# First loads of a hybrid decoder step: sample and shift rows requested by ScalarE, first weights behind the prompt rows, eight extra transposes on TensorE

## What is computed

```python
h = rmsnorm(x, norm_mix)                 # 256 prompt rows, 64 sample rows
proj = h @ w_in                          # (1024 x 3840)
p_prev = state_shift @ w_in[:, HG_COLS:] # 8 rows of the state, not normalised again
# HGRN2 heads and RWKV-7 heads on proj; concatenated; @ w_out; residual
# rmsnorm; router; top 4 of 32 experts, clamped SwiGLU; residual; final rmsnorm
```

## Time and profile before

| | |
|---|---|
| median of 3 runs | 1215.04 us (1213.81 to 1215.45) |
| span of the profiled execution | 1212.7 us |
| PE busy | 1189.5 us, 98% of the span |
| PEld, DVE, ACT, POOL busy | 47%, 37%, 22%, 4% of the span |
| DMA | 436.11 MB, mean 360 GB/s |
| chain that ended last | PE 88%, DMA 10%, DVE 1%, issue 1% |

### The profile page before, as it was taken

One profiled execution on the slowest core, in us unless ns is written; L12 is line 12 of the kernel. 1 busy time (PEld: TensorE's weight loads), 2 busy tenths in 40 slices (PEclk: granted clock), 3 DMA queues, 4 the chain that ended last, 5 costly groups with the idle time before them and its releaser, 6 DMA issues.

```text
span 1212.7 us, 18289 instructions
## 1 busy us (share of the span) xinstructions
PE 1189.5 (98%) x7828; PEld 575.3 (47%) x7828; DVE 446.8 (37%) x967; ACT 260.8 (22%) x637; POOL 43.9 (4%) x101
## 2 busy tenths in 40 slices
PE   8999999999999999999999999999999999999996
PEld 6777777745344344444443444344444444343332
DVE  3367865753313332332233132313322333222324
ACT  3114425522221111111121112021111111111213
POOL 8000110100000000000000000000000000000000
PEclk9999999999999999999999999999999999999999
DMA  9832312498999999999999999999999999999996
GB/s 286 182 105 70 98 54 72 140 403 321 408 429 427 424 415 430 425 434 430 429 432 431 430 430 432 431 432 430 429 432 431 430 431 431 430 430 430 424 422 236
DMA packets 49388, 436.11 MB, mean 360 GB/s; under 512 B 11525, under 2 KB 26952, under 8 KB 31770
## 3 DMA queue, kind: packets, MB, share of 16 engines
q1 hardware_dynamic: 48180, 431.74, 86.3%
q0 software_dynamic: 960, 3.02, 0.8%
q10 hardware_dynamic: 166, 0.15, 0.0%
HBM read 430.01 MB, written 4.89 MB: 359 GB/s over the span
## 4 chain that ended last, share of the span: by engine, by line
PE 88%; DMA 10%; DVE 1%; issue 1%; ACT 0%; SPq 0%; DVEq 0%
PE bank L1623 33%; PE bank L1659 16%; PE bank L913 10%; PE bank L1589 7%; DMA ring<-in_w_gate_up 4%; PE bank L1693 4%; PE bank L1384 3%; DMA ring<-in_w_down 3%; PE bank L1650 3%; DMA mix<-in_w_gate_up 2%; PE bank L1684 1%; PE bank L1141 1%; PE bank L900 1%; PE bank L946 1%; PE bank L1115 0%
## 5 line engine op out<-in xcount | busy, mean ns | idle before, releaser
L1623 PE MATMUL bank<-ring,mix 128*64 128x512 f32 x1504 | 344.8, 598 | 3.1 <-DMA ring<-in_w_gate_up 2.7
L1623 PEld LDWEIGHTS bank<-ring,mix 128*64 128x64 f32 x1504 | 101.3, 136 | 200.8 <-issue 197.3
L1659 PE MATMUL bank<-ring,mix 128*64 128x512 f32 x736 | 168.2, 598 | 0.9 <-DMA ring<-in_w_down 0.8
L2974 DVE TENSOR_TENSOR hTb<-bank,w2a 128x512 f32<-128x512 f32 x32 | 22.1, 692 | 361.1 <-PE bank L1650 361.1
L913 PE MATMUL bank<-hTb,ring 128*128 128x328 f32 (+1 forms) x416 | 119.8, 441 | 1.9 <-issue 1.3
L2210 ACT ACTIVATE mix<-bank,nf 128x256 f32<-128x256 f32 x64 | 26.8, 470 | 430.5 <-PE bank L1589 430.5
L1623 PE MATMUL bank<-mix 128*64 128x512 f32 x500 | 112.7, 595 | 1.6 <-DMA mix<-in_w_gate_up 1.6
L3034 DVE TENSOR_TENSOR mix<-mix,bank 128x512 f32<-128x512 f32 x70 | 48.2, 688 | 159.4 <-PE bank L1693 143.5
L913 PEld LDWEIGHTS bank<-hTb,ring 128*128 128x128 f32 x416 | 77.1, 190 | 35.8 <-issue 3.3
L1659 PEld LDWEIGHTS bank<-ring,mix 128*64 128x64 f32 x736 | 49.5, 136 | 89.9 <-issue 83.9
L1623 PEld LDWEIGHTS bank<-mix 128*64 128x64 f32 x500 | 35.1, 137 | 71.6 <-issue 70.2
(11 more groups left out here) (450 smaller groups left out, 1100.0 us busy)
## 6 DMA issues: line engine op xcount, KB each, us to landing
ring<-in_w_gate_up SPq DMA_DIRECT2D x30, 4096.0 KB, 22.5
ring<-in_w_gate_up SPq DMA_DIRECT2D x33, 2048.0 KB, 14.1
ring<-in_w_down SPq DMA_DIRECT2D x15, 4096.0 KB, 23.3
mix<-in_w_gate_up SPq DMA_DIRECT2D x10, 4096.0 KB, 23.4
ring<-in_w_down SPq DMA_DIRECT2D x14, 2048.0 KB, 13.6
mix<-in_w_gate_up SPq DMA_DIRECT2D x11, 2048.0 KB, 13.0
mix<-in_w_down SPq DMA_DIRECT2D x5, 4096.0 KB, 24.7
ring<-in_w_in SPq DMA_DIRECT2D x14, 1024.0 KB, 5.7
```

The costliest lines, as they stand in the source:

```text
L1623: last_ = mm(b_[64 * half:64 * half + 64, :].rearrange("s (p q) -> s p q", q=4), toks, cols[:, half], start=(c == 0), stop=(c == KT - 1))
L1659: last_ = mm(b_[r:r + 64, :], lhs, w[:, o:o + NCOL], start=(j == 0 and q == 0), stop=(j == 1 and q == 3))
```

## The change

SyncE no longer requests the sample and shift rows; it requests the two halves of the first weight chunk directly behind the prompt rows. ScalarE requests norm_mix, then the shift rows, then the sample rows, and only after its one-element Sqrt the rows norm_ffn and rw_mu. The four other parameter rows that ScalarE had requested (w0, a0, r_k and the HGRN2 norm gain) are now requested by SyncE, behind the two weight halves and ahead of its own six. The number of requests that count up each semaphore is the same.

TensorE gets eight transposes of `ones` whose results nobody reads: four into bank 5 ahead of its wait for norm_mix, four into bank 6 behind norm_mix's transpose and ahead of the wait for row tile 0. Each is a weight load of 128 x 128 and a pass of 128 columns.

```diff
--- before.py
+++ after.py
@@ -591,12 +591,14 @@
             xp, xs = A["x_prompt"], A["x_sample"]
             load(h[:, 0, :], xp[0, 0:P, :], "x0_wo0_in")
             load(h[:, 1, :], xp[0, P:2 * P, :], "x1_wo1_in")
-            load(h[0:64, 2, :], xs.rearrange("b t d -> (b t) d"), "x_in")
-            load(h[64:72, 2, :], A["state_shift"][0], "x_in")
             w_in = A["w_in"][0].rearrange("(c p) n -> p c n", p=P)
             g, u = WORDER[0]
             for x in range(2):
                 load(slot(0)[:, 4 * x:4 * x + 4, :], w_in[:, 4 * x:4 * x + 4, 512 * g + 256 * u:512 * g + 256 * u + 256], ("ring0", "w00_bdr_in")[x])
+            for nm, src in (("w0", "rw_w0"), ("a0", "rw_a0")):
+                params(nm, A[src].rearrange("a (h p) -> (a h) p", p=P))
+            params("rk", A["rw_r_k"][0].rearrange("(j h) n -> j (h n)", h=2))
+            params("gnw", A["hg_norm_w"])
             params("lb0", A["lb_logits"][0:1, :].rearrange("a (h p) -> (a h) p", p=P))
             params("lb1", A["lb_logits"][1:2, :].rearrange("a (h p) -> (a h) p", p=P))
             for nm, src in (("kk", "rw_k_k"), ("ka", "rw_k_a"), ("lnw", "rw_lnx_w"), ("lnb", "rw_lnx_b")):
@@ -876,8 +878,12 @@
                                             ident[0:tn_, 0:tn_])
                 if tile_ == 2:
                     filled(last_, "hT")
+            for k in range(4):
+                nc.tensor.transpose(banks[5][:, P * k:P * k + P], ones[:, :], ident[:, :])
             pe.wait_ge(S("nm_brow_in"), 16)
             filled(nc.tensor.transpose(bank("nmT", 0)[:, 0:KT], prow[0:KT, :], ident[0:KT, 0:KT]), "nmT")
+            for k in range(4):
+                nc.tensor.transpose(banks[6][:, P * k:P * k + P], ones[:, :], ident[:, :])
             for tile in range(3):
                 pe.wait_ge(S(("x0_wo0_in", "x1_wo1_in", "x_in")[tile]), (16, 16, 32)[tile])
                 for c in range(KT):
@@ -1972,16 +1978,17 @@
             def ready(ins, stage):
                 ins.then_inc(S(f"{stage}_ready"), 1)
 
-            for nm, src in (("nm", A["norm_mix"].rearrange("a (c p) -> (a c) p", p=P)),
-                            ("nf", A["norm_ffn"].rearrange("a (c p) -> (a c) p", p=P)),
-                            ("mu", A["rw_mu"].rearrange("a (h p) -> (a h) p", p=P)),
-                            ("w0", A["rw_w0"].rearrange("a (h p) -> (a h) p", p=P)),
-                            ("a0", A["rw_a0"].rearrange("a (h p) -> (a h) p", p=P)),
-                            ("rk", A["rw_r_k"][0].rearrange("(j h) n -> j (h n)", h=2)), ("gnw", A["hg_norm_w"])):
+            def params(nm, src, name):
+
                 n0, k = PR[nm]
-                act.dma_start(prow[n0:n0 + k, :], src).then_inc(S("nm_brow_in" if nm == "nm" else "prow_in"), 16)
+                act.dma_start(prow[n0:n0 + k, :], src.rearrange("a (c p) -> (a c) p", p=P)).then_inc(S(name), 16)
+            params("nm", A["norm_mix"], "nm_brow_in")
+            act.dma_start(h[64:72, 2, :], A["state_shift"][0]).then_inc(S("x_in"), 16)
+            act.dma_start(h[0:64, 2, :], A["x_sample"].rearrange("b t d -> (b t) d")).then_inc(S("x_in"), 16)
             act.wait_ge(S("params_ready"), 1)
             a(st[0:1, 12:13], st[0:1, 12:13], ACT.Sqrt)
+            params("nf", A["norm_ffn"], "prow_in")
+            params("mu", A["rw_mu"], "prow_in")
             for tile in range(3):
                 r = TN[tile]
                 act.wait_ge(S(("x0_wo0_in", "x1_wo1_in", "x_in")[tile]), (16, 16, 32)[tile])
```

## The result

The changed kernel takes 1220.07 us, median of six runs (1217.36 to 1222.84); the kernel before, on the same chips, 1215.24 (1213.81 to 1216.4). The ratio is 1.0041, 95% interval 1.0031 to 1.0051: slower by about 4.8 us, where the prediction had 0.5 us faster and a range that ended at 1216.0. The span of the profiled execution is 1219.4 us against 1212.7.

A forecast was written before the change was run, and what follows sets the result against it. PE and full DMA engines bound the expert stage, started by PE's progress. The smaller of 0.55 (ScalarE) and 0.57 (weights), rounded to 0.5, with parameter rows and transposes at 0, took 1215.04 to 1214.5 us; range 1212.8 to 1216.0.

The forecast's parts named there:

- What bounds the kernel; a shift of the start reaches the end.: Whole kernel: PE and DMA full in the expert stage, so a PE shift at 12 us reaches the end one for one.
- falls into another step: Expert stage: a small shift could change who waits on whom, 1.64 us allowed either way; chance 0.07.
- ACT's queue: Start, ScalarE: table load near 2.57 instead of 3.59, first Square 4.64 instead of 5.00, third Square up to 1.07 us earlier.
- The rows: Start: sample and shift rows come beside prompt tile 1, third Square between 6.72 and 7.84; gain 1.07 to nothing, middle 0.55.
- The weights; the cap of 0.57: First projection: first weight half lands 0.2 us earlier, at 8.85, capping the gain of step c=1 at 0.57 us.
- The parameter rows, 0: SyncE's last parameter request goes out about 0.3 us later, without delaying PE's line 968; 0 in the sum.
- Eight idle transposes cost 0: Start, PE: both idle gaps before 4.14 us hold the transposes; cost 0, at most 0.1 us on tile 0.
- What the transposes bring: Start, PE: earlier clock rise, prompt transposes' weight loads down from 231 to 141 ns; worth 0 to 0.15 us.
- a clock that stays low: Rival at the prompt transposes: clock stays low despite early PE work, c=1 near 9.6, -0.35 us, 1214.7; chance 0.03.
- The rival on the slower side: Parameter rows land after 12.04 and line 967's wait stops PE; +0.3 us, 1215.3; chance 0.10.
- the forecast's sign: Whole kernel: predicted faster, -0.5 us on 1215.04.

The follow-up runs named there:

- one-queue run: Kernel before with both halves of the first weights requested ahead of the sample and shift rows, all on SyncE's queue, no transposes; 1220.26 us, 1.0038.
- the run with the order mended: Changed kernel with the four small parameter requests ahead of the two weight halves on SyncE's queue, eight full idle transposes kept; 1217.9 us, 1.0015.
- the nine runs of the table: Kernel before, changed kernel and seven variants of requests or idle transposes, compared at the idle time near 197 us; ratios from 0.9995 (four small) to 1.0048 (sixteen small).

## Why the prediction was wrong

- *What bounds the kernel; a shift of the start reaches the end.* Right in the main. The changed kernel was 4.76 us late at the start, 4.97 at the group of 126, and the expert stage kept its length, so the rival "falls into another step" did not happen. But it isn't one for one, and the stretch before 230 us has slack: of 2.77 us with the requests alone, 1.67 were left at the group and 1.0 at the end.
- *ACT's queue.* Right in direction: table load at 2.33 (forecast 2.57), first Square at 4.15 (forecast 4.64), second at 5.91. The 0.66 us for the two requests behind the Sqrt were not paid: they went out from 2.40 to 3.22, beside the table load.
- *The rows.* **This step failed.** It said that the sample and shift rows are "fetched beside tile 1 and not behind it", and put the third Square between 6.72 and 7.84; it started at 10.32. I weighed what the rows do to tile 1 and never what the weights, moved ahead at the same moment, do to the rows. The one-queue run (order alone: 1.0038) and the run with the weights 1.6 us later (1.0001) show it. The same sentence on "bytes ahead" that I used for the weights' landing should have been applied to the rows: 512 KB of weights asked for 0.04 us ahead of them and 512 KB more 0.44 us behind. The Trainium skill's rule that I cited (DMA: Bandwidth & Descriptors, "Issuing engines are not separate DMA queues", requests of several engines run on the same 16 DMA engines) spoke for this, and the landing at 10.3 agrees; I used it on the wrong transfer.
- *The weights; the cap of 0.57.* **Failed as well.** I had the first half 0.2 us earlier, at 8.85, on the grounds that the bytes ahead of it are the same. It landed near 10.3, 1.3 us later than before; in the two other kernels with these requests (requests alone, eighteen more transposes) at 9.5 and 9.7. From 10.3 step c=1 can't start before 10.8, against 9.97 before, so this alone turns the forecast gain into a loss.
- *The parameter rows, 0.* Right; PE passed the parameter transpose (line 974) without a wait. The test is weak, as everything ahead of it was 4.76 us later.
- *Eight idle transposes cost 0.* **Failed.** At their own place they are free, as said (the tokens' first transpose starts at 4.18 against 4.14). Their 16 places in PE's program are what the run with them alone shows as its loss, 1.0024. I had counted every DMA that an edit issues, but not its instructions as bytes of a program that is fetched while the DMA queues are full. The idle time of 0.90 us labelled "issue" stood in the trace of before; the earlier trace rows held it among 2.9 us that I passed over.
- *What the transposes bring.* Not settled. PE's weight loads of prompt tile 1, first with the transposes alone, then in the kernel after:

```profile
5.98 0.86 PEld L875 LDWEIGHTS bank<-idg,hx 128*128 128x128 f32 x8 [0.27 <-DMA hx<-in_x_prompt]
```

```profile
5.93 1.29 PEld L877 LDWEIGHTS bank<-idg,hx 128*128 128x128 f32 x8 [0.19 <-DMA hx<-in_x_prompt]
```

  The mean of one is 141 and 194 ns, against 231 in the earlier trace rows. So the clock was up from about 6 and 7 us. But with the same eight transposes it rose at 7.5, 8.5 and 13.5 us in three other kernels, with four, eight and sixteen small ones at 8.9, 7.0 and 7.9, and without any at 7.8 to 9.1 in the five kernels whose start is that of before: one execution of each doesn't show that the transposes did it. The Trainium skill's rule (TensorE: Matmul & The Clock Gate, "Part 4: PE-mode transpose", transposes leave the clock low) fits neither of the two rows above, where only transposes had run, though in the run with the order mended the clock did stay low.
- *The clock.* **Missing.** I priced a clock that stays low, but not one that falls after a wait. It is low at both places: about 2.2 us at the start, and after the far idle time twelve passes take 5.09 us where they took 0.29 each before (3.4 in all): 1.6 us.
- *The rival on the slower side* had the wrong mechanism and 0.3 us; none of my cases reached 4.8.

The two parts together: requests 1.0025 and transposes 1.0024, against 1.0041 [1.0031, 1.0051] for both. That the forecast's sign was wrong is thus two separate misses: the landing of the rows (and weights), and a term put at 0, the transposes' place in the program.

## What to carry to other kernels

Before a transfer is moved ahead, list what is asked for within the same microsecond, on every queue, and ask what each of them now does to the others; moving two things forward can move one of them back, and here moved both. Instructions added ahead of a long program are not free because they run in an idle time: look for short idle times labelled "issue" and for a packet of the instruction queue that lands just ahead of their ends. There they are edges of fetched blocks, and what is added ahead of them can lengthen them, above all where the DMA engines are full. And price a wait of PE with what the clock takes after it.

## What the runs showed of the hardware

- PE's program is fetched in blocks of 16 KB, and PE goes on 1.2 to 1.6 us after a block's packet has landed (47 idle times in eighteen traces). Beside transfers at 360 GB/s the packet started 3.5 us after the group's start, and PE could go on 5.7 to 6.3 us after it, in the nine runs of the table; with the DMA share at 0.15 the next packet started 1.4 us after its block's start, and PE could go on after 4.1. A block with less work than that makes PE stand, up to 4.33 us in the table.
- Idle times of 0.84 to 1.38 us left the passes behind them at 0.30 us each (five in 1.51); those of 1.90 us and more were followed by passes of 0.42 to 0.53 us at a granted clock of 0.50 for part of the way.
- Sixteen nops of PE did not move the edge of a block; eight transposes of 8x8 moved it as far as eight of 128x128.
- 4 KB of norm_mix took 5.49 us behind 256 KB on the same queue.
- Transfers asked for together on two queues were late together: asked for within 0.8 us of each other, the first half of 1 MB of weights and 288 KB of rows landed near 10.3 us (9.5 in one and 9.7 to 9.9 in another kernel with these requests), where before, with the rows asked for ahead of the weights on one queue, the first half of the weights had landed at 9.0 and the rows at 7.8.
- Left open: why a start with the same idle transposes was warm at 6 to 7 us in two kernels and not before 14 in a third, and why the clock fell again near 10.4 us in the run with eight small transposes, where PE had waited at most 0.6 us.
